# Block 1's mixing projections: fp32 matmuls replaced by three fp32r products of upper and lower parts

## The reference, cut to what matters

```python
u = rmsnorm(h, norm_mix[i]) @ w_mix_in[i]
z, xbc, dt_raw, q, k, v, q_idx, k_idx, w_idx = jnp.split(u, SPLIT_POINTS, axis=-1)
y_ssd = ssd_mixer(z, xbc, dt_raw, ...)   # convolution, scan over 16 heads, gate, norm
y_att = dsa_mixer(q, k, v, q_idx, k_idx, w_idx, positions)   # index logits, top 64, 8 heads
h = h + jnp.concatenate([y_ssd, y_att], axis=-1) @ w_mix_out[i]
```

## Time and profile before

| | us |
|---|---|
| median of 3 runs | 2895.63 (2885.95 to 2902.95) |
| profiled execution, its own time | 2894.85 |
| its span in the trace | 2893.0 |
| mean granted TensorE clock | 0.987 |
| layer 0: norm and mixing | 211.7 to 547.7 |
| layer 1: norm and mixing | 927.1 to about 1260.5 |

### The profile page before, as it was taken

The page is one execution under the profiler, slowest core; times in us unless marked ns, Lnnn a source line. Parts: engine busy times, 40 slices in busy tenths (PEclk is TensorE's granted clock), DMA queues, the critical chain, the costliest instruction groups (busy, mean ns, idle before and its releaser), DMA issues.

```text
span 2893.0 us, 37806 instructions
## 1 busy us (share of the span) xinstructions
PE 2789.4 (96%) x15990; PEld 2317.2 (80%) x15990; DVE 1711.3 (59%) x2391; ACT 1156.9 (40%) x1515; POOL 388.7 (13%) x331
## 2 busy tenths in 40 slices
PE   7999999999999999999999999999999979899998
PEld 6888777888888867788878766767878869788887
DVE  7843235586784223458589743347757659655674
ACT  5431313444442121344433545524434433565443
POOL 2400010131230001023102410010000000521000
PEclk9999999999999999999999999999999999999999
DMA  7563585455555467545513221225555524344652
GB/s 226 184 193 118 180 257 181 144 190 189 174 181 170 136 202 253 167 151 186 179 59 105 77 81 59 59 88 195 177 167 184 181 73 144 109 125 120 208 188 100
DMA packets 442319, 445.09 MB, mean 154 GB/s; under 512 B 13711, under 2 KB 433672, under 8 KB 442150
## 3 DMA queue, kind: packets, MB, share of 16 engines
q1 hardware_dynamic: 438878, 436.52, 47.2%
q0 software_dynamic: 2400, 5.40, 0.9%
q10 hardware_dynamic: 872, 0.75, 0.1%
HBM read 441.46 MB, written 1.17 MB: 153 GB/s over the span
## 4 chain that ended last, share of the span: by engine, by line
PE 89%; DVE 7%; ACT 3%; DMA 1%; issue 1%; SPq 0%; ACTq 0%; DVEq 0%
PE bank L1563 29%; PE bank L1564 15%; PE bank L1662 13%; PE bank L1525 12%; PE bank L1672 7%; PE bank L1558 2%; DVE R L2583 2%; PE bank L1778 2%; PE bank L1986 1%; PE bank L1720 1%; PE bank L1977 1%; DVE lower L2130 1%; DVE lower L689 1%; ACT upper L1037 1%; PE bank L1848 1%; PE bank L1890 1%
## 5 line engine op out<-in xcount | busy, mean ns | idle before, releaser
L1563 PE MATMUL bank<-h_pair,upper 128*128 128x512 f32 x2464 | 877.2, 401 | 30.8 <-DVE h_pair L2161 18.7
L2130 DVE TENSOR_TENSOR lower<-ring,upper 128x2048 fp32r<-128x2048 f32 (+1 forms) x238 | 567.4, 2386 | 291.7 <-ACT upper L1037 291.6
L1564 PE MATMUL bank<-h_pair,lower 128*128 128x256 f32 x2464 | 693.5, 281 | 0.0
L1037 ACT ACTIVATE upper<-ring 128x2048 fp32r<-128x2048 f32 (+1 forms) x238 | 441.6, 1863 | 484.6 <-PE bank L1564 483.1
L1563 PEld LDWEIGHTS bank<-h_pair,upper 128*128 128x128 f32 x2464 | 467.6, 190 | 147.4 <-issue 28.2
L1564 PEld LDWEIGHTS bank<-h_pair,lower 128*128 128x128 f32 x2464 | 469.8, 191 | 0.2
L1563 PE MATMUL bank<-hid_pair,upper 128*128 128x512 f32 x1232 | 432.8, 396 | 0.0
L1564 PE MATMUL bank<-hid_pair,lower 128*128 128x256 f32 x1232 | 344.7, 280 | 0.0
L1563 PEld LDWEIGHTS bank<-hid_pair,upper 128*128 128x128 f32 x1232 | 231.2, 188 | 55.4
L1662 PE MATMUL bank<-hT,ring 128*128 128x256 f32 x1152 | 254.5, 383 | 6.9 <-DVE hT L2089 6.0
L1662 PEld LDWEIGHTS bank<-hT,ring 128*128 128x128 f32 x1152 | 220.8, 192 | 39.0 <-issue 6.7
(11 more groups left out here) (312 smaller groups left out, 3608.7 us busy)
## 6 DMA issues: line engine op xcount, KB each, us to landing
ring<-in_w_ffn_in SPq DMA_DIRECT2D x154, 1024.0 KB, 5.1
ring<-in_w_ffn_out SPq DMA_DIRECT2D x56, 1024.0 KB, 4.9
ring<-in_w_mix_in SPq DMA_DIRECT2D x48, 1024.0 KB, 5.3
ring<-in_w_mod SPq DMA_DIRECT2D x48, 1024.0 KB, 6.2
ring<-in_w_in SPq DMA_DIRECT2D x42, 1024.0 KB, 5.1
ring<-in_w_ffn_out SPq DMA_DIRECT2D x28, 768.0 KB, 4.2
ring<-in_w_mix_out SPq DMA_DIRECT2D x16, 1024.0 KB, 5.7
ring<-in_w_in SPq DMA_DIRECT2D x16, 512.0 KB, 5.3
```

The costliest lines, as they stand in the source:

```text
L1037: act.activation(f.upper(p)[:, 0:n], slot[:, 0:n], ACT.Copy).then_inc(up_ready, 1)
L1563: pe.matmul(bank[:, 0:2 * T], up[:, cols], x_pair.rearrange("p e t -> p (e t)"), start=first, stop=False)
L1564: return pe.matmul(bank[:, 0:T], low[:, cols], x_pair[:, 0, :], start=False, stop=last)
L2130: dve.tensor_tensor(f.lower(p)[:, 0:n], slot[:, 0:n], f.upper(p)[:, 0:n].bitcast(F32), ALU.subtract)\
```

## The change

All matmuls of block 1's mixing except the mods become three fp32r products. `plan_pieces` gives each of these pieces an upper buffer (`uppers1`, the three of the FFNs and two more in `R`) and the item that frees it. On ACT `split1_up` waits for the piece's landing and for the upper buffer, and copies; on DVE `split1_low` waits for that and subtracts; TensorE waits for `low1_ready` (`split1`). These calls are put into the lists by hand: pieces 0 and 1 in the last thirds of FFN1, a piece of (2) three items ahead, qkv piece n + 2 right behind the eviction of qkv item n, output piece 0 before the y norm, the others one unit ahead, the last behind the units. The normed x is made whole, rounded by ACT and subtracted by DVE (`mixing_h`); `ysT` and the attention output are split too, the latter straight out of `M[3]`, where now DVE's subtract signals `o_ready`. `ysT`, `yaT` and `mod_rows` get other places in SBUF. TensorE waits twice for `ys_ready`, one half each.

```diff
         self.slot, self.use, self.before = slot, use, before
-        self.n, self.up, self.up_before = None, None, None
+        self.n, self.up, self.up_before, self.width = None, None, None, SLOT
...
-        for name, i, end in LAYER1:
+        for n, (name, i, end) in enumerate(LAYER1):
             add(name, i, l, ("third", end[1] + l * 2 * THIRDS) if isinstance(end, tuple) else end + l * ITEMS1,
                 len(out) % NW)
+            piece = out[-1]
+            if name == "mod":
+                continue
+            if name.startswith("ffn"):
+                p = n if n < FF_PIECES else n - FF2_PIECE
+                up = ((2 * l + (n >= FF_PIECES)) * FF_PIECES + p) % NUP
+            elif name == "qkv":
+                up = min((1, 2), key=lambda r: up_held[r][0])
+            elif name == "mix_out":
+                up = MIXO_UPPERS[i % 3]
+            else:
+                up = ((2 * l + 1) * FF_PIECES + n - MIX_PIECE) % NUP
+                piece.width = KD * {"dt": SSD_H, "kw": N_KW}.get(name, PC)
+            turn += 1
+            if not name.startswith("ffn"):
+                piece.n, piece.up, piece.up_before = mixed1, up, up_held.get(up, (0, None))[1]
+                mixed1 += 1
+            up_held[up] = (turn, piece.end)
...
         uppers = [over("upper0", "Q", 0, SLOT), over("upper1", "sq", 0, SLOT), over("upper2", "sq", SLOT, SLOT)]
...
-        ysT, yaT = hT[:, 1], hT[:, 0]
+        ysT = R[:, 0:2048].rearrange("p (c t) -> p c t", c=KD)
+        ys_pair = over("ys_pair", "hT", 0, 2 * KD * T).rearrange("p (c e t) -> p c e t", c=KD, e=2)
+        ya_pair = over("ya_pair", "R", 3120, 2 * KD * T).rearrange("p (c e t) -> p c e t", c=KD, e=2)
...
+        def split1_low(eng, pos):
+
+            piece = PIECES[pos]
+            eng.wait_ge(up1_ready, piece.n + 1)
+            w = piece.width
+            eng.tensor_tensor(lowers[piece.slot][:, 0:w], slots[piece.slot][:, 0:w],
+                              uppers1[piece.up][:, 0:w].bitcast(F32), ALU.subtract).then_inc(low1_ready, 1)
...
+            def split1_up(pos):
+
+                piece = PIECES[pos]
+                has_landed(act, pos)
+                if piece.up_before is not None:
+                    ended(act, piece.up_before)
+                w = piece.width
+                act.activation(uppers1[piece.up][:, 0:w], slots[piece.slot][:, 0:w], ACT.Copy).then_inc(up1_ready, 1)
...
+                    elif f.mix is not None and p + 1 < FF_PIECES:
+                        split1_up(f.mix + p + NUP - FF_PIECES)
...
-            def out_unit(u0, i, dst, rows_, n):
+            def out_unit(u0, i, dst):
                 act.wait_ge(o_filled, (u0 + (i + 1)))
-                act.activation(dst, M[3][rows_, 0:n], ACT.Copy).then_inc(o_ready, 1)
+                act.activation(dst, M[3][:, 0:T], ACT.Copy).then_inc(ya_up_ready, 1)
...
+                mixp = poss + MIX_PIECE
+                for c in range(KD):
+                    act.wait_ge(h1_whole_ready, l * KD + c + 1)
+                    act.activation(h_up[:, c, :], h_whole[:, c, :], ACT.Copy).then_inc(h1_up_ready, 1)
+                split1_up(mixp + 2)
                 for i in range(6):
...
+                    split1_up(mixp + i + 3)
+                split1_up(mixp + 9)
                 it = mix + 7
...
+                split1_up(mixp + 10)
...
                     filled(act, it)
                     take_item(it, [(idxt[:, :, PC * i:PC * (i + 1)], token_halves(banks(it)[0]))])
+                    split1_up(mixp + 11 + i)
...
+                    if i == 0:
+                        split1_up(mixp + 13)
+                    elif i >= 2:
+                        split1_up(poss + FILL_PIECE["qkv", i - 2])
...
                         if what == "qkv":
                             take_item(it, [(qkv[:, :, PC * n:PC * (n + 1)], token_halves(banks(it)[0]))])
+                            if n + 2 < len(QKV_AT):
+                                split1_up(poss + FILL_PIECE[what, n + 2])
...
                         take_fills("head", 2 * i + e)
+                split1_up(poss + MIXO_PIECE)
...
                     if i < ATT_H:
                         exp_unit(u0, i)
+                    if i < 2:
+                        act.wait_ge(ys_whole_ready, 2 * l + i + 1)
+                        c = slice(4 * i, 4 * i + 4)
+                        act.activation(ys_pair[:, c, 0, :], ysT[:, c, :], ACT.Copy).then_inc(ys_up_ready, 1)
+                    elif 4 <= i < ATT_H + 2:
+                        split1_up(poss + MIXO_PIECE + i - 3)
                     take_fills("unit", i - 1)
                     if 2 <= i < ATT_H + 2:
                         turn_unit(u0, i - 2)
                     if i >= 3:
-                        out_unit(u0, i - 3, yaT[:, i - 3, :], slice(0, P), T)
+                        out_unit(u0, i - 3, ya_pair[:, i - 3, 0, :])
+                split1_up(poss + MIXO_PIECE + 7)
...
+            def split1(pos):
+
+                piece = PIECES[pos]
+                pe.wait_ge(low1_ready, piece.n + 1)
+                return uppers1[piece.up], lowers[piece.slot]
+
+            def form1_a(it, w, cols):
+
+                bank = start_item(it)
+                up, low = w
+                for s in range(2):
+                    o, tokens = bank[0][:, cols * s:cols * (s + 1)], slice(128 * s, 128 * (s + 1))
+                    for k in range(KD):
+                        c = slice(k * cols, (k + 1) * cols)
+                        for n, (x_, w_) in enumerate(((h_up, up), (h_low, up), (h_up, low))):
+                            mm = pe.matmul(o, x_[:, k, tokens], w_[:, c], start=k == 0 and n == 0,
+                                           stop=k == KD - 1 and n == 2)
+                mm.then_inc(gemm_filled, 1)
...
+                        w = split1(poss + (MIX_PIECE + n))
                         if name in ("xbc", "z"):
-                            form_b(mix + n, w, lambda k: hT[:, 0, k, :], PC, KD, T,
+                            form2_b(mix + n, w, lambda k: (h_up[:, k, :], h_low[:, k, :]), PC, KD, T,
                                    before_k=(lambda k: pe.wait_ge(h_ready, (norm + 1) * KD + k + 1)) if n == 0 else None)
                         else:
-                            form_a(mix + n, w, {"dt": SSD_H, "kw": N_KW}.get(name, PC), 2)
+                            form1_a(mix + n, w, {"dt": SSD_H, "kw": N_KW}.get(name, PC))
...
                 def mixer_output(n, src):
 
-                    form_b(items + (MIXO_ITEM + n), arrived(poss + (MIXO_PIECE + n)), lambda k: src[:, k, :], PC, KD, T)
+                    form2_b(items + (MIXO_ITEM + n), split1(poss + (MIXO_PIECE + n)),
+                            lambda k: (src[:, k, 0, :], src[:, k, 1, :]), PC, KD, T)
...
-                            form_a(it, arrived(poss + FILL_PIECE[what, n]), PC, 2)
+                            form1_a(it, split1(poss + FILL_PIECE[what, n]), PC)
...
-                            pe.wait_ge(ys_ready, (l + 1))
-                        mixer_output(MIXO_AT_UNITS.index(i), ysT)
+                            pe.wait_ge(ys_ready, 2 * (l + 1))
+                        mixer_output(MIXO_AT_UNITS.index(i), ys_pair)
...
-            def normed(n, gain, nh, chain, dst, signal, scaled=None):
-
-                dve.wait_ge(root_ready, (n + 1))
-                chain(dve.reciprocal(root[:, 0:nh * T], root[:, 0:nh * T]))
+            def mixing_h(l, n, gain, chain):
+
+                dve.wait_ge(root_ready, n + 1)
+                chain(dve.reciprocal(root[:, 0:T], root[:, 0:T]))
                 chain.settle()
+
+                def low_part(c):
+                    dve.wait_ge(h1_up_ready, l * KD + c + 1)
+                    dve.tensor_tensor(h_low[:, c, :], h_whole[:, c, :], h_up[:, c, :].bitcast(F32), ALU.subtract)\
+                       .then_inc(h_ready, 1)
+
                 for c in range(KD):
-                    for hf in range(nh):
-                        ins = dve.scalar_tensor_tensor(out=dst[:, hf, c, :], in0=xT[:, hf, c, :],
-                                                       scalar=gain(c, hf), in1=root[:, hf * T:(hf + 1) * T],
-                                                       op0=ALU.mult, op1=ALU.mult)
-                    ins.then_inc(signal, 1)
+                    dve.scalar_tensor_tensor(out=h_whole[:, c, :], in0=xT[:, 0, c, :], scalar=gain(c, 0),
+                                             in1=root[:, 0:T], op0=ALU.mult, op1=ALU.mult).then_inc(h1_whole_ready, 1)
+                    if c >= 2:
+                        low_part(c - 2)
+                for c in range(KD - 2, KD):
+                    low_part(c)
...
+                elif f.mix is not None and p + 1 < FF_PIECES:
+                    split1_low(dve, f.mix + p_to)
...
-                normed(norm + 1, gain("norm_mix"), 1, chain, hT, h_ready)
-
-                dve.wait_ge(pad_ready, (l + 1))
-                for c0 in range(0, KC1, 4):
```

(59 more changed lines are left out.)

12 lines of the change are left out of this document (9 added, 3 removed).

## The result

The changed kernel takes **2950.08 us**, median of four runs (2945.6 to 2953.58), against 2893.93 for the kernel before in the same series: a ratio of 1.0192, with a 95% interval of 1.0158 to 1.0227. It is slower by 1.9%. The forecast of 2903 us, no difference, was wrong, and the range of 2868 to 2932 did not hold the time. The profiled execution took 2953.58 us, with a span of 2951.8 at a mean granted clock of 0.963; before, the clock was 0.987.

A forecast was written before the change was run, and what follows sets the result against it. TensorE, busy 96% of the span, was taken as the bound. Products at -39.6 us a layer plus added costs, waits and clock falls gave +4.2 a layer, +8.4 for two, on 2894.85: 2903 us, range 2868 to 2932.

The forecast's parts named there:

- the narrow items: dt (16 columns) and kw (72): 96 matmuls at 0.115 us cost 11.0, +3.7 us a layer.
- the falls of the clock in the heads: Behind stalls at qkv items 7, 8 and 9, the granted clock falls three times: +5.4 us a layer.
- the wait ahead of the logits: Between z items and logits: qkv piece 1's upper part on ACT precedes three index copies, +1.9 us a layer.
- the entry of the units: Start of the attention units: a low filling DVE's idle time and two half-piece ys lows, +1.9 us a layer.
- The products: Mixing's 256-column items: form_a from 7.10 to 5.76 us, form_b from 6.91 to 5.75, -39.6 us a layer.
- The start: Start of the mixing: two more writes and a subtract before the first chunk of hT releases TensorE, +1.3 us.
- The pass count's 27 us: Skill's four passes for FP32 against one: items fall a quarter to 5.33 us, total some 27 us lower.
- The mechanism: ACT waits for loads into just-freed slots, stalling TensorE: +4.8 us in the logits, +13.6 in the heads, a layer.
- the +0.4 for the queue: Other qkv pieces in the heads, five or fewer behind: the load queue keeps up within +0.4 us a layer.
- The tail: Last score product to output item 4, +5.5 us a layer; start of FFN2, +0.7.
- The half of a fall: In the tail the clock may fall; half of 1.8 us charged, +0.9 a layer.
- Rival three: Slower: the eight loads ACT waits for land later; at 8.7 instead of 5.3 us, +27, 2930 us; chance 0.28.

The follow-up runs named there:

- k2_ahead_one: Changed kernel with every qkv piece's upper part made one qkv item ahead and before the eviction, instead of two ahead and behind it; lower parts move too: 2868.33 us.
- k3_wide: Changed kernel with the dt and kw products given 256 columns each in place of 16 and 72: 2935.88 us.
- k5_warm: Changed kernel with six unread fp32 products put ahead of TensorE's waits in three places of the heads of each layer: 2932.88 us.
- k1_first_q: Changed kernel with only qkv piece 1's split moved: upper part ahead of qkv item 0's eviction, lower part behind the third block of scores: 2935.77 us.
- k11_three_entry: Changed kernel with qkv split one item ahead, dt and kw 256 columns wide, tail splits moved, output piece 0's upper part behind ScalarE's squares: 2834.90 us.
- k4_tail: Changed kernel with output pieces 5 and 6 split behind the attention units, 7 behind the first residual, FFN2's first splits between the last output items: 2929.70 us.

## Why the prediction was wrong

The changed kernel is dearer than the sum by 23 us in layer 0 and 26 in layer 1. The steps that failed are four terms, each 8 to 10 us too low over both layers: the narrow items, the falls of the clock in the heads, the wait ahead of the logits, and the entry of the units.

**The products: right, nearly.** The z items take 5.76, form_a's 5.95 where I had 5.76: 0.2 too low for 14 items a layer. The start (+1.35 for +1.3), the xbc and z stretches, output items 0 to 2 and, in layer 0, the tail up to item 4 came within 0.3 us. The pass count's 27 us in the prediction takes 5.33 for both forms; a quarter off form_b's 6.91 is 5.18, which makes it 33. No item came near either.

**The mechanism: right.** ScalarE, held by a load whose slot the item just evicted had freed, holds the mod evictions and relu behind it. It is named as foreseen behind the logit item and three items of the heads, and leaves TensorE empty for 4.69, 6.39, 3.93 and 4.83 us in layer 0, where 4.8, 4.9, 3.8 and 4.9 were forecast. k2_ahead_one takes it away, and the time with it.

**"The narrow items, +3.7": failed, by 10 us over both layers.** dt and kw took 6.7 more in layer 0 and 10.9 in layer 1. The 0.115 a record of the earlier trace rows is layer 1's, where the clock stayed at 1.00. In layer 0 the kernel before already had the fall, and kw took 6.3 us for the earlier trace rows's 3.8, in the same view of the groups:

```profile
L1672 PE MATMUL bank<-ring,hT 128*128 128x72 f32 x32 | 6.3, 387 | 0.0
```

I read one layer of two and took it for the price of a narrow product. The 11.0 us of the forecast are what the widened products of k3_wide take at full clock; the narrow ones take 16.7 and 18.3, for the clock falls beside them in both layers.

**"Three falls of the clock, +5.4": mis-sized, by 8.** I took the 1.8 us behind the gap of 3 us for all gaps. The three in the heads of layer 0 come to 10.1: 3.3 behind 6.39 us of idle time, 2.4 (an item of 8.30) behind 3.93, 4.4 (turn, row product and an item of 8.52) behind 4.83; those of layer 1 come to 9.1. The cost does not follow the length of the gap. It follows how long the low level lasts once TensorE works again, 7.3, 5.2 and 9.8 us here and about 3 in the earlier trace rows, and costs about half of that. k5_warm takes out 14 us in both layers. The landing of 6.81 in place of 5.3 adds 1.5 at one gap, and ten items at 5.95 add 1.9. With the 4.7 of the clock, less the +0.4 for the queue, which did not come, these make the 7.8 by which the stretch lost more than foreseen.

**"But the up of qkv piece 1 sits on ACT ahead of the three index copies: +1.9": a wait overlooked.** I charged the upper part and not the load in front of it. The rule that I applied to the logits, a slot freed by the sixth piece before, holds here too: it is the last z item. The load of 5.73 us stands in the chain, the stretch grew by 6.1 where 1.9 was foreseen, and the clock is low behind it; the edit k1_first_q gives 14 us back.

**The entry of the units, +1.9: failed by 4.** ScalarE makes output piece 0's upper part ahead of the squares that TensorE sums, so its 1.91 us stands in the chain (`474.14 1.91`), and the sums that follow run in part at the low clock, 5.4 us for 4.1. I had given only VectorE's lower part a price there. k11_three_entry, which moves this one operation, shortens the stretch by 3.2.

**The tail: 1.8 short.** The chain from output item 4 to FFN2's first product holds three items in 19.79 us, with the clock low until 550; at k4_tail's 5.8 each they would take 17.4. The half of a fall that I charged, 0.9, was 2.4.

**The rivals.** Rival three, slower, came true in its sign and not by its reason: the ten waits for a load in the chain are 5.3 to 7.1 us, 5.75 on average, where the forecast had 5.35: some 4 us of the 56. The rest was the narrow items, the clock, and a load and an upper part not counted. The Trainium skill, "TensorE: Matmul & The Clock Gate", section "HAM oscillation — how this bites in real kernels", describes a kernel which waits for a load between short bursts of products and starts each burst at the low clock. The trace agrees for the five places of layer 0, where the first products behind the load run at 0.50. The prediction charged each of its places 1.8 us, which is not the whole of what follows at the low clock.

## What to carry to other kernels

When faster products need a second form of their operand, the copy joins an engine that works in order, and what counts is where in that order it stands. Put it ahead of the eviction that waits anyway, and at a distance at which its load has long landed. Behind every stall of some us, charge also the products that follow it at half clock: 2.4 to 4.4 us here behind gaps of 3.9 to 6.4, where one row with a gap of 3 had said 1.8. Take the length of a gap from TensorE's timeline, for the chain leaves out what runs beside a wait. And read a duration in every layer with its granted clock before it goes into a sum: kw's 3.8 us was 6.3 in the other layer.

## What the runs showed that was not expected

The granted clock fell beside products of few columns although TensorE is marked busy throughout. With 16 and 72 columns the granted clock of layer 0 was 0.50 from 258 to 270 us, with 256 columns 1.00, and qidx, dt and kw together took 22.9 us for 28.6 and 30.2. The Trainium skill, "TensorE: Matmul & The Clock Gate", section "What's actually happening", ties the clock to how busy the engine has been; by that rule these windows, busy for 4.00 of 4.00 us, would have run at full speed. The measurement decides: they ran at 0.50. Why, the runs do not show. It is not every narrow product, for the same two items ran at 1.00 in layer 1 of the kernel before; and that dt and kw were widened together leaves open which of the two matters.

Six dummy products in a gap kept the clock at 1.00 for what followed. They cost nothing in the gap that was longer than their 5.35 us, and 0.5 and 1.5 us in the two that were shorter. As a bandage they are worth 14 us; taking the waits away is worth 78.
